# Block kernel of one core: order of VectorE at the change of the token half, one load ahead of a store, bank waits one by one

## What is computed

```python
def swiglu(h, w_gate, w_up, w_down):
    return (jax.nn.silu(h @ w_gate) * (h @ w_up)) @ w_down

    x = x + rms_norm(mix, norm_mix_post[l])
    f = swiglu(rms_norm(x, norm_ffn_pre[l]), w_gate[l], w_up[l], w_down[l])
    x = x + rms_norm(f, norm_ffn_post[l])
```

## Time and profile before

| | us |
|---|---|
| median of three runs | 1917.43 (1917.12 to 1918.08) |
| the profiled execution, its time | 1919.53 |
| its span in the trace | 1917.7 |
| PE busy | 1866.2 (97%) |
| DVE busy | 1178.6 (61%) |
| ACT busy | 711.6 (37%) |
| POOL busy | 560.8 (29%) |

### The profile page before, as it was taken

One profiled execution on the slowest core, in us unless ns is written; L12 is line 12 of the kernel. 1 busy time (PEld: TensorE's weight loads), 2 busy tenths in 40 slices (PEclk: granted clock), 3 DMA queues, 4 the chain that ended last, 5 costly groups with the idle time before them and its releaser, 6 DMA issues. The chain is left out here.

```text
span 1917.7 us, 25255 instructions
## 1 busy us (share of the span) xinstructions
PE 1866.2 (97%) x9464; PEld 1545.9 (81%) x9464; DVE 1178.6 (61%) x1286; ACT 711.6 (37%) x1169; POOL 560.8 (29%) x406
## 2 busy tenths in 40 slices
PE   7999999989999899999999899999999899999998
PEld 5888888878888788888888688888887788888886
DVE  5444444464546877677767867677767546554564
ACT  6555555453335432323234333323333122222342
POOL 2222222220002444444444444444442000000243
PEclk9999999999999999999999999999999999999999
DMA  7111111044574434233326333233324853445665
GB/s 274 67 66 66 66 66 55 33 179 178 206 275 183 171 103 130 87 104 98 126 82 221 119 108 117 82 104 116 108 82 151 335 212 126 174 167 187 228 206 180
DMA packets 128966, 270.26 MB, mean 141 GB/s; under 512 B 5920, under 2 KB 84768, under 8 KB 119456
## 3 DMA queue, kind: packets, MB, share of 16 engines
q1 hardware_dynamic: 128928, 269.78, 40.3%
HBM read 189.54 MB, written 80.22 MB: 141 GB/s over the span
## 5 line engine op out<-in xcount | busy, mean ns | idle before, releaser
L1220 PE MATMUL T<-tb_hi,sb_hi 128*128 128x512 f32 x616 | 240.9, 391 | 7.1 <-DVE sb_lo L1133 7.1
L1221 PE MATMUL T<-tb_lo,sb_hi 128*128 128x512 f32 x616 | 240.2, 390 | 0.0
L1222 PE MATMUL T<-tb_hi,sb_lo 128*128 128x512 f32 x616 | 240.2, 390 | 0.0
L1018 DVE TENSOR_TENSOR t_lo<-t_raw,t_hi 128x1536 fp32r<-128x1536 f32 x132 | 223.8, 1749 | 0.0
L807 ACT ACTIVATE sb_hi<-sb_raw 128x1408 fp32r<-128x1408 f32 x56 | 77.4, 1381 | 299.1 <-PE T L1222 259.5
L571 POOL TENSOR_TENSOR v<-u,p 128x512 f32<-128x512 f32 x44 | 116.2, 2640 | 183.4 <-DVE u L1042 158.3
L1397 PE MATMUL T<-s_hi,t_hi 128*128 128x512 f32 x352 | 138.6, 394 | 6.4 <-DVE s_lo L1011 4.5
L555 POOL TENSOR_TENSOR t_raw<-t_raw 128x512 f32<-128x512 f32 x44 | 60.8, 1381 | 281.1 <-DMA t_raw<-w_gu 281.1
L1220 PEld LDWEIGHTS T<-tb_hi,sb_hi 128*128 128x128 f32 x616 | 116.0, 188 | 32.9 <-issue 8.2
L1399 PE MATMUL T<-s_hi,t_lo 128*128 128x512 f32 x352 | 138.4, 393 | 0.0
L1398 PE MATMUL T<-s_lo,t_hi 128*128 128x512 f32 x352 | 138.0, 392 | 0.0
(11 more groups left out here) (194 smaller groups left out, 4522.4 us busy)
## 6 DMA issues: line engine op xcount, KB each, us to landing
t_raw<-w_gu SPq DMA_DIRECT2D x44, 1024.0 KB, 4.8
act_d<-ac SPq DMA_DIRECT2D x22, 1792.0 KB, 8.0
sb_raw<-act_d SPq DMA_DIRECT2D x56, 704.0 KB, 4.1
h_d<-quarters SPq DMA_DIRECT2D x8, 1792.0 KB, 6.6
s_raw<-h_d SPq DMA_DIRECT2D x14, 1024.0 KB, 8.1
tb_raw<-w_dn SPq DMA_DIRECT2D x6, 1536.0 KB, 6.3
hT_raw<-x_t SPq DMA_DIRECT2D x16, 512.0 KB, 3.2
xt<-x SPq DMA_DIRECT2D x16, 512.0 KB, 3.9
```

What stands on the lines that cost most here:

```text
L1018: e.tensor_tensor(t_lo[u][:, first:end, :], t_raw[u][:, first:end, :], t_hi[u][:, first - 1:end - 1, :].bitcast(F32), ALU.subtract).then_i ...
L1220: e.matmul(out_ap, lhi, rhi, start=start, stop=False)
L1221: e.matmul(out_ap, lhi, rlo, start=False, stop=False)
L1222: return e.matmul(out_ap, llo, rhi, start=False, stop=stop)
```

## The change

Three things are edited. On DVE, at the change of the block, the `lower` and the `gated` of pass 21 and the four sums of group 10 move against the splits of `s` and the `chain` and `t_lo` of the next passes. On SP, at the start of the down phase, the load of the third block's operand is issued ahead of the last `act_store`, and the load of the fifth block waits for `act_out`. On PE, a pass no longer waits at its start for all four `silu` or `gated` of the pass two before it: its first product waits for two of them (bank 0 is then read out), the second for `v12_done`, the fourth for `v21_done`.

```diff
--- before.py
+++ after.py
@@ -437,14 +437,17 @@
             load_sb(0)
             e.wait_ge(prod_done, 7 * (2 * GROUPS - 1) + 5)
             load_sb(1)
-            act_store(GROUPS - 1)
             e.wait_ge(prod_done, 14 * GROUPS)
             for it in range(7 * TILES // 2):
                 i, m = it // (TILES // 2), it % (TILES // 2)
+                if it + 2 == BP:
+                    e.wait_ge(act_out, 16 * GROUPS)
                 if it + 2 < 7 * TILES // 2:
                     load_sb(it + 2)
                 if m == 0 and 0 < i < 6:
                     e.wait_ge(dn_done, TILES // 2 * i)
+                if it == 0:
+                    act_store(GROUPS - 1)
                 if i == 0:
                     if m < 2:
                         load_tb(1, 1, 1, m)
@@ -453,7 +456,6 @@
                         e.wait_ge(tb_sum, m - 2)
                         load_sub(1, 0, 0, m - 3)
                     if m == 2:
-                        e.wait_ge(act_out, 16 * GROUPS)
                         e.dma_start(postf[:, :], post_ffn).then_inc(post_in, 16)
                 if i == 1 and m < 2:
                     load_tb(2, 1, 1, m)
@@ -1058,13 +1060,21 @@
                 e.scalar_tensor_tensor(out=ac[:, slot, :], in0=ac[:, slot, :], scalar=0.5, in1=src,
                                        op0=ALU.mult, op1=ALU.mult).then_inc(act_done, 1)
 
-            def group_end(g, next_block):
-                lower(2 * g + 1, 1)
+            def gated_start(g):
+                e.wait_ge(sil_done, 4 * g + 4)
+                e.wait_ge(v22_done, 2 * g + 2)
+                gated(3, v22[:, :])
+                e.wait_ge(prod_done, 14 * g + 12)
+                gated(1, GU[1][0])
+
+            def upper_end(g):
+                upper(2 * g + 1, 1)
+                e.wait_ge(v12_done, 2 * g + 2)
+                gated(2, v12[:, :])
+
+            def gated_end(g):
                 e.wait_ge(v21_done, 2 * g + 2)
                 gated(0, v21[:, :])
-                if next_block:
-                    for i in range(4, 7):
-                        s_lo_part(next_block, i)
                 e.wait_ge(act_done, 4 * g + 4)
                 e.tensor_tensor(ac[:, 4, :], ac[:, 0, :], ac[:, 3, :], ALU.add).then_inc(act_sums, 1)
                 e.tensor_tensor(ac[:, 6, :], ac[:, 1, :], ac[:, 0, :], ALU.subtract).then_inc(act_sums, 1)
@@ -1082,10 +1092,17 @@
                     pair_sums(TILES // 2 - 1)
                     s_lo_part(0, 5)
                     s_lo_part(0, 6)
+                elif first:
+                    s_lo_part(b, 5)
+                    s_lo_part(b, 6)
+                    e.wait_ge(v21_done, n)
                 else:
-                    group_end(g - 1, b if first else 0)
+                    lower(n - 1, 1)
+                    gated_end(g - 1)
                 chain(n, 0)
                 t_lo_parts(n + 1, 1)
+                if first and not begin:
+                    gated_end(g - 1)
                 if begin:
                     e.wait_ge(h2_out, 8 * TILES)
                 else:
@@ -1106,20 +1123,17 @@
                 if switch:
                     s_lo_part(b + 1, 0)
                     s_lo_part(b + 1, 1)
-                e.wait_ge(sil_done, 4 * g + 4)
-                e.wait_ge(v22_done, n + 2)
-                gated(3, v22[:, :])
-                e.wait_ge(prod_done, 7 * n + 12)
-                gated(1, GU[1][0])
+                gated_start(g)
                 if switch:
                     s_lo_part(b + 1, 2)
-                upper(n + 1, 1)
-                e.wait_ge(v12_done, n + 2)
-                gated(2, v12[:, :])
+                    s_lo_part(b + 1, 3)
+                upper_end(g)
                 if switch:
-                    s_lo_part(b + 1, 3)
+                    lower(n + 1, 1)
+                    s_lo_part(b + 1, 4)
                 if final:
-                    group_end(g, 0)
+                    lower(n + 1, 1)
+                    gated_end(g)
 
             half = [slice(0, 6), slice(6, NG)]
 
@@ -1373,8 +1387,10 @@
 
             def up_half(n, g, u, first, begin):
                 for i, (s, t) in enumerate(UP_PRODUCTS):
-                    if i == 0 and not begin:
-                        e.wait_ge((sil_done, act_done)[u], 4 * g)
+                    if not begin and i == 0:
+                        e.wait_ge((sil_done, act_done)[u], 4 * g - 2)
+                    if not begin and i in (1, 3):
+                        e.wait_ge((v12_done, v21_done)[i // 2], n - 1)
                     if i < 3:
                         e.wait_ge(t_split, 3 * n + i + 1)
                     if first and u == 0:
```

## The result

| | before | changed |
|---|---|---|
| median us (lowest, highest, runs) | 1917.55 (1917.12, 1921.72, 8) | 1924.90 (1922.71, 1925.87, 8) |
| ratio, 95% interval | | 1.0032, 1.0022 to 1.0041 |
| profiled execution: time, span | 1919.53, 1917.7 | 1925.46, 1923.7 |
| pass 22's start to pass 24's start | 47.65 | 53.42 |
| pass 24's start to down block 0 | 382.31 | 382.31 |

The change makes the kernel slower, by 0.32%, that is 6.1 us (4.2 to 7.9). The two medians are 7.35 us apart, which lies within that interval. The last three rows are differences of matmul starts in the two traces. They say at once where the time is: 5.77 us at the change of the block, nothing between, 0.43 in the down phase. (The changed kernel reached pass 22 0.23 us earlier: 5.77 + 0.43 - 0.23 = 5.97, the distance of the last matmuls.)

A forecast was written before the change was run, and what follows sets the result against it. PE was taken as the bound, busy 1866.2 of 1917.7 us. Late store +2.9, clock +1.65, bank waits 0 and down phase -0.5 gave +4.05 on 1917.43, so 1921.5, range 1917.3 to 1923.8.

The forecast's parts named there:

- (a): Pass 22, DVE's new order: `u3` starts at 1071.6 and pass 23 at 1075.2 in place of 1080.48, 5.3 us won.
- (b): Behind `u3`: the late store delays `silu` and ACT's copy; product 4 of pass 23 stands about 8.1 us, 2.9 lost.
- U: The start of `u3` in pass 22, put at 1071.6, from which the store and all behind it were reckoned.
- The clock at the block change: Pass 23: PE's clock falls to its lower level after the stall of 8.1 us, 1.65 us lost.
- the hand-on: Pass 24: its `t0` load is issued 6 us later behind the store, but just hidden; otherwise a few tenths.
- worse: Rival: the block-change delay is handed on through pass 24's operand or POOL's `corner`, +6 to +9 us, 1925; chance 0.08.
- No net change: Rival: gain and loss at the block change even out, with `u3` near 1069.5; 1917.4 us, chance 0.05.
- faster: Rival: the first `silu` after the block change does not wait for the late store; 1911.6 us, chance 0.08.
- Smaller bill: Rival: same stall, but the clock holds after one stall or the store lands 2 us sooner; 1919.5 to 1919.8, chance 0.22.
- line rate: Store of group 10: by the 512 B rule it takes 4.2 us in place of 6.2, sum +2.05; not adopted.
- (c): PE's bank waits: nothing won, cost 0, at most 0.02 us for each of some 80, 1.6 in all.
- (d): Down phase: PE's stall of 5.4 us moves from block 2 to block 3; block 4 starts 0.5 us earlier.

The follow-up runs named there:

- e11: Changed kernel, with GpSimd waiting for the four `silu` of group 11 before its sums of the weights for pass 24; ratio 1.0036 to the kernel before.
- e10: Kernel before, with only the late multiplication and four sums of group 10 behind `t_lo` and the bank waits this needs; ratio 1.0039.
- e8: Kernel before, with only the changed bank waits of PE; ratio 0.9996.
- e1: Kernel before, with only SP's edit (third operand of the down phase loaded ahead of the last store); ratio 1.0000.
- e5: Changed kernel, with the multiplication and four sums of group 10 between `chain` and `t_lo`; ratio 1.0006 to the kernel before.
- e6: Kernel before with SP's edit, and the down phase's fourth and fifth operands issued ahead of the loads of the weights; ratio 0.9962, median 1911.37 us.
- e2: Changed kernel, with the multiplication and four sums of group 10 again ahead of `u2` and `u3`; ratio 1.0007 to the kernel before.
- e3: Changed kernel, with group 10's store in two DMAs, the first ahead of the sums, and `silu` waiting only for that; ratio 1.0012 to the kernel before.

## Why the prediction came out as it did

The forecast was 1921.5 in 1917.3 to 1923.8, slower with a chance of 0.5. The direction and the mechanism were right: 0.32% slower, by a stall before product 4 of pass 23, for ACT's copy, for `silu`, for the late store. On the median of before that the forecast started from, the ratio gives 1923.6, near the upper end; the changed kernel's own median, 1924.90, lies 1.1 above it. The loss was 6.1 us and not 4.05, and part of the difference is scatter of the clock, as the sum below shows. By its own steps:

**(a) Head of pass 22.** `u3` was put at 1071.6 and started at 1071.61 (pass 22 itself began 0.23 earlier, so 0.24 late in this measure). Product 6 at 1072.5: 1072.44. Pass 23 at 1075.2: 1075.25. `s_lo3` was better than computed (product 3 had no wait) and product 4's wait shorter (1.41 and not 3.3), which changed nothing, since `u3` came last.

**(b) What comes behind it.** The store was put at U + 9.0 and left at U + 9.01 (1080.62 - 1071.61). It held DVE for 8.68 us, put at 8.47. From there to the end of the copy are 1095.36 - 1089.30 = 6.06 us, put at 5.04. This is the term that was mis-sized most: "Now it takes from 1083.05 to 1087.51 + 0.58 = 1088.09, 5.04 us". I took over the chain's length as it was and did not ask what would run beside it, although the same part of the prediction says that GpSimd's sums move with the load. VectorE's third and fourth `silu` and GpSimd's first sum in the kernel before show how near they stood:

```profile
1085.64 0.69 DVE L1054 SCALAR_TENSOR_TENSOR ac<-th,v 128x512 f32<-128x512 f32 x1 [0.70 <-ACT th L756]
...
1087.63 1.67 DVE L1054 SCALAR_TENSOR_TENSOR ac<-th,v 128x512 f32<-128x512 f32 x1 [0.70 <-ACT th L756]
```

```profile
1086.16 1.33 POOL L555 TENSOR_TENSOR t_raw<-t_raw 128x512 f32<-128x512 f32 x1 [7.43 <-DMA t_raw<-w_gu]
```

The third `silu`, the last ahead of the copy, began 0.52 us before GpSimd's sums, and only the fourth, which the copy does not need, met them and took 1.67. The `silu` and the sums both wait for SP's queue and moved together, but not by quite the same: in the changed kernel the sums began 0.09 us before the third `silu` (1091.80 and 1091.89), and it took 1.72 in place of 0.69. e11 holds GpSimd back and the chain is 1.03 shorter. With the 0.2 of the store and the 0.24 of `u3` the term is 4.3 (1095.41 - 1091.36 + 0.23) in place of 2.9.

**The clock at the block change** was put at 1.65 and cost 1.49 in the changed kernel's trace. Its granted clock, by stretches of 2 us (start, end, PE busy, clock, DMA share, GB/s):

```profile
1088.00:1090.00 2.00, 0.00 (x0) 1.00 1.02 360
1090.00:1092.00 2.00, 0.00 (x0) 0.89 0.54 225
1092.00:1094.00 2.00, 0.00 (x0) 0.50 0.00 0
...
1096.00:1098.00 2.00, 2.00 (x6) 0.50 0.03 8
1098.00:1100.00 2.00, 2.00 (x9) 0.91 0.00 0
```

It is still full from 1088 to 1090, in the stall, and falls to the lower of its two levels (1.2 GHz) by 1092, while PE stands. It stays there for some three us after PE's restart at 1095.41. A stall of the same length cost 3.04 in e10.

**(b), the hand-on.** Pass 24 followed without a wait, as computed. The rival "worse" did not come: the loss of 6.1 us touches its +6, but nothing was handed on. "No net change" needed `u3` near 1069.5, and it was 1071.61. Nor did "faster": DVE's row with 8.71 us for the store excludes it. "Smaller bill" did not come either: the clock fell after both stalls, and the store was no quicker.

**(b), line rate.** By the rule of 512 bytes that the prediction takes from the Trainium skill, "DMA: Bandwidth & Descriptors", section Specifications, the store would have been 2 us shorter (the prediction's estimate). The trace does not agree: VectorE could go on 8.68 us after the issue, and from 1082 to 1086 the queue moved 290 GB/s at a share of 1.0.

**(c) Bank waits.** Zero within the timing, by e8 and by the 382.31. The upper bound of 0.02 us for each stood in no row.

**(d) Down phase.** The stall moved to block 3, as forecast (TensorE in the changed kernel):

```profile
1487.37 0.47 PE L1234 MATMUL T<-tb_hi,sb_hi 128*128 128x512 f32 x1 [1.35 <-DVE sb_lo L1147]
...
1515.68 0.79 PE L1234 MATMUL T<-tb_hi,sb_hi 128*128 128x512 f32 x1 [5.09 <-DVE sb_lo L1147]
```

The gain of 0.5 became a loss of 0.43 in this trace, because the clock stayed down longer behind a stall that was itself not longer:

```profile
1516.00:1518.00 2.00, 2.00 (x6) 0.50 0.97 409
1518.00:1520.00 2.00, 2.00 (x6) 0.50 1.01 412
1520.00:1522.00 2.00, 2.00 (x7) 0.59 1.10 449
```

The delays of the starts behind the stall add up to 2.91 us here, 1.65 in the kernel before and 1.48 in e1, which has the same edit. So the edit does not force it. In the seven traces with the edit they are 1.5 to 2.9, in the three without 1.6 to 2.3; whether the edit makes a long one more likely stays open. Over the seven traces with the edit (changed, e1 to e5, e11) the down phase is 426.09 to 427.43, mean 426.70; over the three without (before, e8, e10) 426.96 to 427.00. The edit is worth 0.3 us on the mean, with a scatter larger than that, and nothing that the timing can tell. That 1.7 us of queue and not 5.6 were to be had was about right: block 3 began 1515.68 - 1487.37 = 28.31 us after block 0, 1.9 sooner than before (30.21) and put at 28.5. e6 shows the other side: what held the blocks was the place in the queue.

**The sum** in the trace: 4.3 + 1.5 + 0.4 - 0.23 = 6.0, put at 4.05. Of the missing 1.9 us, 1.4 are the chain beside GpSimd, the store and `u3`, and 0.9 the down phase with its longer low clock; against these stand 0.2 of the clock at the block change and the 0.23 by which pass 22 began earlier.

## What to carry to other kernels

When work is put off, ask who waits for its result and also who stands behind that one on each in-order engine. Here the wait of VectorE for a DMA was harmless at 2 us and decided the change at 8.7, and the engine named by PE's wait (ACT) was two hand-ons away from it. And before you take over a chain's length, look at what its neighbours do within a us of it: here two chains that hang on the same queue moved together, and a shift of 0.6 us between them cost 1.0. In this full DMA queue the order of the loads was worth more than an earlier issue: taking 0.7 MB out gave 0.3 us, which the timing cannot tell from nothing, and sorting by first use gave 6.

## What the hardware showed that I had not expected

The price of the lower clock after a stall is not fixed. In the thirteen traces PE has sixteen idle times of 4.8 to 9.1 us at the block change and in the down phase, and behind them the starts were late by 1.4 to 3.0 us, not ordered by the length of the idle time: 1.42 after 4.97 (e2), 2.94 after 4.95 (e2), 1.49 after 9.12 (the changed kernel) and 3.04 after 9.13 (e10). In e3 it also came 1.4 us after PE had started again, behind only 3.25 us of idling, and in e6 behind 1.96. So an edit that leaves a stall where it was can move the time by over 1 us from one execution to the next.

VectorE's sums of 128x512 with both inputs in SBUF took 0.69 us alone and 1.66 to 1.77 with GpSimd's sums or its `corner` beside them. An operation that read PSUM kept its 0.68: in the changed kernel `v21` (L1052) at 1093.53, with GpSimd's sum of 1093.01 beside it.
